# Mamba-2 block on one core: GpSimd's product of conv and D moves ahead of xs, and the decays' subtractions are split in two in the first and last group

## The chip, the cores and the metric

The kernel runs on one core of a Trainium2 chip. The metric is device time in microseconds (us), the median of several executions. TensorE is called PE, VectorE DVE, ScalarE ACT and GpSimd POOL, as in the profile; SP issues most transfers.

## The reference, cut to what matters

The model has two layers; the change lies in the first, a Mamba-2 mixer of 8 groups with 8 heads each:

```python
zxbcdt = u @ in_proj
xbc = silu(causal_depthwise_conv(xbc, conv_w, conv_b))   # x, B and C of the group
a = d * A; cum = cumsum(a)
seg = cum[:, :, None] - cum[:, None, :]
decay = where(causal, exp(where(causal, seg, 0.0)), 0.0)
cb = einsum("bign,bjgn->bijg", c, b)
y_intra = einsum("bijg,bijgr,bjgr,bjgrp->bigrp", cb, decay, d, x)
y_inter = einsum("bign,bgrpn,bigr->bigrp", c, state, exp(cum))
to_end = exp(cum[:, -1:] - cum) * d
y = y_intra + y_inter + D_skip[:, :, None] * xs
g = y * silu(z)                                          # then a group norm and out_proj
```

256 tokens are two chunks of 128. An MLP, a differential attention and another MLP follow and are not touched.

## The kernel before, in words

All large products are made of weights that stream in as slabs of 128x1024 float32. SP loads slab `s` into one of four `raw` buffers; ACT copies its high part (`split`, L622), DVE subtracts it from the original to get the low part (`split`, L912), and PE makes three matmuls for each pair of tiles (`three`, L1445 to L1447). PE takes 24 matmuls of 256 columns for a slab. There are four split buffers (`LEAD`), so ACT may start slab `s` once PE has finished slab `s - 4`, and SP may refill a `raw` buffer once DVE has split it.

The order of everything is written by hand. Each engine goes through the same list of steps `(unit, i)`, one slab a step; at step `k` ACT and DVE first split slab `k + 4` and then do the step's other work (`steps`, `mix_step`); PE multiplies slab `k` and then does the step's other work. An engine runs its own list strictly in order. What a step's other work waits for is a semaphore.

A group's steps are xs (8 slabs), bc (4), z (8) and acc (8, `out_proj` of the group before). The first group has no acc, and the last has z ahead of acc. Where z comes right behind bc (`z_first`), the chain of one group is this, by step:

- (xs, 7) and (bc, 3): DVE's `convolve` of xs and of bc (L1215, L1219); in the first group that of xs is done at (bc, 1). ACT's silu of xs (L769) raises `silu_done` the first time, its silu of bc at (z, 0) (L774) the second.
- (z, 1): DVE's 16 subtractions for the decays (L1245), then `seg_done`.
- (z, 3): PE's `spread` (L1604, L1609) waits for both silus and turns xs; ACT copies it out (L787, `xs_ready`). DVE then makes `bt` and `cbm` (L1254, L1255) and raises `cb_ready`.
- POOL: `xd = xs * dt` for two chunks (L569), `xe` (L575), `yg = conv * D` (L579), then `pool_ready`.
- (z, 4): ACT's exponentials of the decays; DVE's products with `cbm` (L1262).
- (z, 6): PE's product for the state (L1666) waits for `cb_ready` and `pool_ready`. (z, 7): PE's products within the chunk (L1674) and from the state (L1678).

In the six groups of the loop the 16 subtractions stand at (xs, 4), ACT's exponentials at (acc, 3), and `spread` at (acc, 7), where PE also waits for DVE's sum of (acc, 5) (L992, `acc_added`).

Of the kernel before, what the change touches and what calls it, by code (L numbers as in the profile page):

```python
# [25 lines left out]
ALU = mybir.AluOpType  # L26
# [5 lines left out]
S = 256  # L32
MT = S // P
DI = 2 * D
G = 8
# [151 lines left out]
def column_bcast(ap, n):  # L187

    return ap.unsqueeze(2).to_broadcast([ap.shape[0], ap.shape[1], n])
# [7 lines left out]
def build(nc, w, out):  # L197
# [41 lines left out]
    with ctx:  # L239
# [54 lines left out]
        conv = mb("conv", [P, 6, S])  # L294
        xs = mb("xs", [P, MT, BLK])
        xd = mb("xd", [P, MT, BLK])
        xe = mb("xe", [P, BLK])
        yg = mb("yg", [P, 4, S])
# [16 lines left out]
        dcol = mb("dcol", [P, NH // 2])  # L315
# [56 lines left out]
        pre_ready, conv_done, silu_done = sem("pre_ready"), sem("conv_done"), sem("silu_done")  # L372
# [114 lines left out]
        @block.gpsimd  # L487
        def _(pool):
            chain = Tally(pool, pool_chain)
            g_ = nc.gpsimd  # L490

            g_.memset(pre[:, :, 0:TAPS - 1], 0.0)
            g_.memset(ones[:, :], 1.0)
            chain.mark(g_.memset(ident[:, :], 0.0))
            chain.mark(g_.memset(causal[:, :], 1.0))
            chain.wait()
            g_.affine_select(out=ident[:, :], in_=ident[:, :], compare_op=ALU.not_equal, fill=1.0, base=0,
                             pattern=[[-1, P]], channel_multiplier=1)

            g_.affine_select(out=causal[:, :], in_=causal[:, :], compare_op=ALU.is_ge, fill=0.0, base=0,  # L500
                             pattern=[[1, P]], channel_multiplier=-1).then_inc(consts_ready, 1)

            pool.wait_ge(x_in[PIECES - 1], 16)
            for i, name in enumerate(("a_dt_bias", "a_A_log", "a_D")):
                pool.dma_start(hd[:, i, :], w[name][0].partition_broadcast(P)).then_inc(heads_in, 16)
            for i, name in enumerate(("b_lambda_q1", "b_lambda_k1", "b_lambda_q2", "b_lambda_k2")):
                pool.dma_start(lamv[:, i, :], w[name][0].partition_broadcast(P)).then_inc(lam_in, 16)
            pool.dma_start(relrow[:, :], w["rel_bias"].rearrange("b h -> h b"), allow_slow_non_contiguous=True)\
                .then_inc(rel_in, 16)


            pool.wait_ge(rel_in, 16)
            bounds = bucket_bounds()
            g_.memset(bias_row[:, 0:P], MASKED)
            for b in range(BUCKETS):
                lo, hi = P + bounds[b], P + bounds[b + 1]
                last = g_.tensor_copy(bias_row[:, lo:hi], relrow[:, b:b + 1].to_broadcast([HEADS, hi - lo]))
            chain.mark(last)
            chain.wait()

            pool.dma_start(bias_dram, bias_row[:, :]).then_inc(bias_out, 16)

            def zero_y(r):
                pool.wait_ge(x_lo, KT // 2 * (r + 1))
                for nt in range(NT):
                    last = g_.memset(y[:, :, nt * BLK:(nt + 1) * BLK], 0.0)
                last.then_inc(y_zeroed, 1)

            def next_postw(r, vec):
                pool.wait_ge(yw_ready, NT * r)  # L530
                pool.dma_start(postw[:, :], vec.partition_broadcast(P)).then_inc(postw_in, 16)

            def sum_squares(g):

                pool.wait_ge(g_sq, g)
                chain.mark(g_.tensor_tensor(out=zs[:, 0:2, :], in0=zs[:, 0:2, :], in1=zs[:, 2:4, :], op=ALU.add))
                chain.wait()
                g_.tensor_tensor(out=zs[:, 0, :], in0=zs[:, 0, :], in1=zs[:, 1, :], op=ALU.add).then_inc(g_added, 1)

            def group(g):  # L540

                if above(g):
                    pool.wait_ge(silu_done, 2 * g)
                for lo, n, at0 in ((0, 4, g * 4), (4, 1, 32 + g), (5, 1, 40 + g)):
                    for tp in range(TAPS + 1):
                        col = P * (1 + tp // 2) + 48 * (tp % 2)
                        last = g_.tensor_copy(cpar[:, tp, lo:lo + n], par[:, bass.ds(col + at0, n)])
                last.then_inc(cpar_ready, 1)
                if above(g):
                    pool.wait_ge(ecb_ready, g)  # L550
                else:
                    pool.wait_ge(expd_ready, 1)
                g_.tensor_copy(gcum[:, :, :], cum[:, :, bass.ds(g * R, R)]).then_inc(gcum_ready, 1)
                if not above(g):
                    pool.wait_ge(cumt_ready, 1)
                    pool.dma_start(cum_dram, cumt[:, :]).then_inc(cum_out, 16)
                    pool.wait_ge(cum_out, 16)

                src = cum_dram[bass.ds(g * R, R), :].rearrange("r s -> (r s)").partition_broadcast(P)
                pool.dma_start(cumb[:, :, :].rearrange("p r s -> p (r s)"), src).then_inc(cumb_in, 16)  # L560

                if above(g):
                    sum_squares(g)
                pool.wait_ge(xs_ready, g + 1)
                if above(g):
                    pool.wait_ge(h_ready, g)
                chain.mark(g_.tensor_copy(gpar[:, :], par[:, bass.ds(80 + g * 4, 4)]))
                for c in range(MT):
                    last = g_.tensor_tensor(  # L569
                        out=xd[:, c, :].rearrange("p (r d) -> p r d", r=R), in0=xs[:, c, :].rearrange("p (r d) -> p r d", r=R),  # L570
                        in1=column_bcast(dt[:, c, bass.ds(g * R, R)], PD), op=ALU.mult)
                    chain.mark(last)
                    if c == 0:
                        chain.wait()
                        g_.tensor_tensor(out=xe[:, :].rearrange("p (r d) -> p r d", r=R),  # L575
                                         in0=xd[:, 0, :].rearrange("p (r d) -> p r d", r=R),
                                         in1=column_bcast(todend[:, bass.ds(g * R, R)], PD),
                                         op=ALU.mult)
                g_.tensor_tensor(out=yg[:, :, :], in0=conv[:, 0:4, :], in1=column_bcast(dcol[:, bass.ds(g * 4, 4)], S),  # L579
                                 op=ALU.mult).then_inc(pool_ready, 1)  # L580

            pool.wait_ge(par_ready, 2)
            group(0)
            pool.dma_start(postw[:, :], w["norm_post_mix"][0].partition_broadcast(P)).then_inc(postw_in, 16)
            zero_y(0)
            with pool.Fori(0, G - 1) as t:
                chain.enter(t, 4)
                group(t + 1)
            chain.leave(G - 1, 4)
            sum_squares(G)  # L590
            next_postw(1, w["norm_post_mlp"][0])
            zero_y(1)
            next_postw(2, w["norm_post_mix"][1])

            def tab_load(g):

                src = bass.AP(tensor=bias_dram.tensor, offset=g * (HG * (P + S)) + 1,
                              ap=[[1, P], [P + S, HG], [1, S]])
                pool.dma_start(tab[:, :, :], src).then_inc(tab_in, 16)

            pool.wait_ge(bias_out, 16)
            pool.wait_ge(h_new, 2 * H_STEPS)
            tab_load(0)
            zero_y(2)
            with pool.Fori(0, QG - 1) as t:
                pool.wait_ge(lg_ready, HG * (t + 1))
                tab_load(t + 1)
            next_postw(3, w["norm_post_mlp"][1])
            zero_y(3)
# [295 lines left out]
        def _(dve):  # L905
            chain = Tally(dve, dve_chain)
# [320 lines left out]
            def mix_step(first, g, unit, i):  # L1227
# [6 lines left out]
                    block_lo(*((last_b if unit == "acc" else (bhi[0], blo[0]))))  # L1234
                if (unit, i) == ("xs", 6) and not first:
                    gate_factor(g)
                if (unit, i) == (("z", 1) if z_first else ("xs", 4)):

                    dve.wait_ge(cumb_in, 16 * (g + 1))
                    dve.wait_ge(gcum_ready, g + 1)  # L1240
                    if not first:
                        dve.wait_ge(y_done, g)
                    for c in range(MT):
                        for r in range(R):
                            last = ve.tensor_scalar(m[:, c, r, :], cumb[:, r, c * P:(c + 1) * P], gcum[:, c, r:r + 1], 0.0,  # L1245
                                                    ALU.subtract, ALU.min)
                    last.then_inc(seg_done, 1)
                if (unit, i) in (("xs", 7), ("bc", 3)) and not (first and unit == "xs"):
                    convolve(first, g, unit)
                if unit == "acc":  # L1250
# [613 lines left out]
```

## Time and profile before

| | |
|---|---|
| median of 3 runs | 2555.12 us (2554.38 to 2555.68) |
| the profiled execution's own time | 2554.14 us |
| its span (first to last instruction) | 2552.5 us |
| PE busy | 2519.7 us, 99% of the span |
| DVE, ACT, POOL busy | 1800.7, 1220.8 and 154.8 us |
| mixer, first group | to about 94 us; each looped group takes 84 us |

The time outside the span is 1.6 us. A busy share says little here: what counts is where PE stands still, and at which granted clock it works (PEclk, 1.00 is 2.4 GHz and 0.50 is 1.2 GHz).

### The profile page before, as it was taken

What the parts mean: (1) busy time and instruction counts of PE and PEld (TensorE: products, weight loads), DVE (VectorE), ACT (ScalarE), POOL (GpSimd) and SP (SyncE); (2) the same over time, 40 slices, a digit from 0 to 9 for tenths busy, and PEclk for the clock granted to TensorE, in tenths of its full rate; (3) what the DMA queues carried; (4) which work ended last, traced back from release to release, by engine and by line L of the source; (5) the groups of instructions that cost most, each with busy time, mean ns of one, the idle gap of its engine ahead of it and who ended that gap; (6) DMA issues with size and microseconds to landing.
All of it is one profiled execution on the core that took longest, in us unless ns stands there. A gap on an engine that the chain in (4) does not pass through costs nothing.

```text
span 2552.5 us, 45617 instructions
## 1 busy us (share of the span) xinstructions
PE 2519.7 (99%) x17261; PEld 2320.2 (91%) x17261; DVE 1800.7 (71%) x2580; ACT 1220.8 (48%) x1597; POOL 154.8 (6%) x269
## 2 busy tenths in 40 slices
PE   8999999999999999999999999999999999999997
PEld 7999999999899989899998998998899999989896
DVE  6878777887886565666666876778866666565667
ACT  6555545554554343434444654455644444343433
POOL 2222022202100000000000000000000000000000
PEclk9999999999999999999999999999999999999999
DMA  7666656656556666666666555555566666666664
GB/s 198 198 203 190 181 179 201 196 174 189 176 173 198 190 190 189 191 192 186 193 181 197 188 176 174 176 172 167 177 192 188 192 182 197 189 190 189 191 191 135
DMA packets 267579, 474.14 MB, mean 186 GB/s; under 512 B 16625, under 2 KB 50530, under 8 KB 265954
## 3 DMA queue, kind: packets, MB, share of 16 engines
q1 hardware_dynamic: 264818, 457.92, 59.3%
q0 software_dynamic: 2624, 15.00, 1.9%
q8 instruction: 57, 0.93, 0.1%
q14 instruction: 32, 0.26, 0.0%
q10 hardware_dynamic: 48, 0.02, 0.0%
HBM read 470.70 MB, written 2.19 MB: 185 GB/s over the span
## 4 chain that ended last, share of the span: by engine, by line
PE 96%; DVE 2%; ACT 1%; issue 0%; DMA 0%; SPq 0%; DVEq 0%; ACTq 0%
PE ps L1445 31%; PE ps L1446 31%; PE ps L1447 31%; PE ps L1674 1%; DVE whl L912 1%; PE ps L1546 0%; PE ps L1762 0%; PE ps L1678 0%; ACT whl L622 0%; DMA h<-x 0%; DVE m L1245 0%; PE ps L1604 0%; PE ps L1666 0%; DVE conv L1219 0%; PE ps L1574 0%
## 5 line engine op out<-in xcount | busy, mean ns | idle before, releaser
L912 DVE TENSOR_TENSOR whl<-raw,whl 128x1024 fp32r<-128x1024 f32 x865 | 1071.4, 1239 | 689.7 <-ACT whl L622 677.2
L622 ACT ACTIVATE whl<-raw 128x1024 fp32r<-128x1024 f32 x865 | 916.5, 1060 | 1173.7 <-PE ps L1447 1165.3
L1445 PE MATMUL ps<-xhl,whl 128*128 128x256 f32 x3588 | 1011.7, 282 | 3.9 <-DVE whl L912 2.0
L1446 PE MATMUL ps<-xhl,whl 128*128 128x256 f32 x3588 | 1001.9, 279 | 0.0
L1447 PE MATMUL ps<-xhl,whl 128*128 128x256 f32 x3588 | 1001.3, 279 | 0.0
L1445 PEld LDWEIGHTS ps<-xhl,whl 128*128 128x128 f32 x3588 | 674.5, 188 | 8.6 <-DVE whl L912 2.2
L1446 PEld LDWEIGHTS ps<-xhl,whl 128*128 128x128 f32 x3588 | 674.6, 188 | 3.1 <-issue 1.9
L1447 PEld LDWEIGHTS ps<-xhl,whl 128*128 128x128 f32 x3588 | 674.3, 188 | 0.0
L1445 PE MATMUL ps<-whl,bhl 128*128 128x512 f32 x1320 | 512.9, 389 | 0.0
L1446 PE MATMUL ps<-whl,bhl 128*128 128x512 f32 x1320 | 512.3, 388 | 0.0
L1447 PE MATMUL ps<-whl,bhl 128*128 128x512 f32 x1320 | 511.9, 388 | 0.0
L1447 PEld LDWEIGHTS ps<-whl,bhl 128*128 128x128 f32 x1320 | 247.8, 188 | 51.3
L1445 PEld LDWEIGHTS ps<-whl,bhl 128*128 128x128 f32 x1320 | 247.9, 188 | 50.1
L1446 PEld LDWEIGHTS ps<-whl,bhl 128*128 128x128 f32 x1320 | 247.8, 188 | 49.5
L996 DVE TENSOR_TENSOR y<-y,ps 128x1024 f32<-128x1024 f32 x141 | 172.1, 1221 | 7.3 <-PE ps L1447 2.5
L823 ACT ACTIVATE bhl<-relu 128x512 fp32r<-128x512 f32 x64 | 36.9, 625 | 83.2 <-DVE relu L1295 83.2
L1445 PE MATMUL ps<-khl,whl 128*128 128x256 f32 x256 | 72.7, 284 | 0.0
L1446 PE MATMUL ps<-khl,whl 128*128 128x256 f32 x256 | 71.5, 279 | 0.0
L1447 PE MATMUL ps<-khl,whl 128*128 128x256 f32 x256 | 71.4, 279 | 0.0
L1445 PE MATMUL ps<-whl,khl 128*128 128x512 f32 (+1 forms) x164 | 64.0, 390 | 0.0
L1447 PE MATMUL ps<-whl,khl 128*128 128x512 f32 (+1 forms) x164 | 63.1, 385 | 0.0
L1446 PE MATMUL ps<-whl,khl 128*128 128x512 f32 (+1 forms) x164 | 63.0, 384 | 0.0
(224 smaller groups left out, 1677.8 us busy)
## 6 DMA issues: line engine op xcount, KB each, us to landing
raw<-mlp_w SPq DMA_DIRECT2D x512, 512.0 KB, 4.2
raw<-a_in_proj SPq DMA_DIRECT2D x161, 512.0 KB, 4.5
raw<-a_out_proj SPq DMA_DIRECT2D x64, 512.0 KB, 4.2
raw<-b_w_q SPq DMA_DIRECT2D x32, 512.0 KB, 3.7
raw<-w_k SPq DMA_DIRECT2D x32, 512.0 KB, 4.0
raw<-w_v SPq DMA_DIRECT2D x32, 512.0 KB, 3.7
raw<-b_out_proj SPq DMA_DIRECT2D x32, 512.0 KB, 3.7
cumb<-cum_scratch POOLq DMA_DIRECT2D x8, 1024.0 KB, 7.7
```

The lines of the kernel that those rows point to most:

```text
L622: sc.activation(whi[:, s.split, lo:lo + SLAB], raw[:, s.raw, :], ACT.Copy).then_inc(hi_ready, 1)
L823: last = sc.activation(bhi[which][:, 2 * n:2 * n + 2, :].rearrange("p f s -> p (f s)"), relu[:, n, :], ACT.Square)
L912: ve.tensor_tensor(out=wlo[:, s.split, lo:lo + SLAB], in0=raw[:, s.raw, :], in1=whi[:, s.split, lo:lo + SLAB].bitcast(F32), op=ALU.subtrac ...
L996: ve.tensor_tensor(out=cols, in0=cols, in1=ps[:, bank:bank + 2, :], op=ALU.add).then_inc(acc_added, 1)
L1445: te.matmul(outs, lh, rh, start=start, stop=False, skip_group_check=True)
L1446: te.matmul(outs, lh, rl, start=False, stop=False, skip_group_check=True)
L1447: return te.matmul(outs, ll, rh, start=False, stop=stop, skip_group_check=True)
L1674: te.matmul(ps[r % 2 * PD:(r % 2 + 1) * PD, 5 + r // 4, col:col + P], xd[:, c, r * PD:(r + 1) * PD], m[:, c, r, :], start=True, stop=True, ...
```

## The change

Two things. POOL makes `yg = conv * D` as soon as the silu of xs is done, ahead of its wait for `xs_ready`; `pool_ready` is now raised by the second `xd`. And where z comes right behind bc (first and last group), DVE makes the eight subtractions of chunk 0 at (z, 1) and those of chunk 1 at (z, 2), so one slab split stands between them.

```diff
@@ POOL, group(g)
-                pool.wait_ge(xs_ready, g + 1)
+                pool.wait_ge(silu_done, 2 * g + 1)
                 if above(g):
                     pool.wait_ge(h_ready, g)
+                g_.tensor_tensor(out=yg[:, :, :], in0=conv[:, 0:4, :], in1=column_bcast(dcol[:, bass.ds(g * 4, 4)], S), op=ALU.mult)
+                pool.wait_ge(xs_ready, g + 1)
                 chain.mark(g_.tensor_copy(gpar[:, :], par[:, bass.ds(80 + g * 4, 4)]))
...
-                    chain.mark(last)
                     if c == 0:
+                        chain.mark(last)
                         chain.wait()
...
-                g_.tensor_tensor(out=yg[:, :, :], in0=conv[:, 0:4, :], in1=column_bcast(dcol[:, bass.ds(g * 4, 4)], S),
-                                 op=ALU.mult).then_inc(pool_ready, 1)
+                last.then_inc(pool_ready, 1)
@@ DVE, mix_step
-                if (unit, i) == (("z", 1) if z_first else ("xs", 4)):
+                if (unit, i) in ((("z", 1), ("z", 2)) if z_first else (("xs", 4),)):
...
-                    for c in range(MT):
+                    for c in (i - 1,) if z_first else range(MT):
...
-                    last.then_inc(seg_done, 1)
+                    if c == MT - 1:
+                        last.then_inc(seg_done, 1)
```

POOL's queue in the first group, `-` before and `+` changed (`yg`, `gpar`, `xd`, `xe` are the tiles written, `postw` the norm weights loaded next):

```order
-L567 COPY gpar<-par 128x4
-L569 TENSOR_TENSOR xd<-xs,dt 128x512
-L575 TENSOR_TENSOR xe<-xd,todend 128x512
-L569 TENSOR_TENSOR xd<-xs,dt 128x512
-L579 TENSOR_TENSOR yg<-conv,dcol 128x1024
-L584 DMA postw<-norm_post_mix 128x2048
+L567 TENSOR_TENSOR yg<-conv,dcol 128x1024
+L569 COPY gpar<-par 128x4
+L571 TENSOR_TENSOR xd<-xs,dt 128x512
+L577 TENSOR_TENSOR xe<-xd,todend 128x512
+L571 TENSOR_TENSOR xd<-xs,dt 128x512
+L585 DMA postw<-norm_post_mix 128x2048
```

The product `yg` stands first instead of last. The same move is made in every group of the loop.

DVE's queue in the first group before, from the slab split of step (z, 1) on:

```order
L912 TENSOR_TENSOR whl<-raw,whl 128x1024
L1245 TENSOR_SCALAR m<-cumb,gcum 128x128 x16
L912 TENSOR_TENSOR whl<-raw,whl 128x1024 x2
L1254 COPY bt<-ps 128x128
L1255 TENSOR_TENSOR cbm<-ps,causal 128x256
```

And changed (its lines are one or two further down):

```order
L913 TENSOR_TENSOR whl<-raw,whl 128x1024
L1246 TENSOR_SCALAR m<-cumb,gcum 128x128 x8
L913 TENSOR_TENSOR whl<-raw,whl 128x1024
L1246 TENSOR_SCALAR m<-cumb,gcum 128x128 x8
L913 TENSOR_TENSOR whl<-raw,whl 128x1024
L1256 COPY bt<-ps 128x128
L1257 TENSOR_TENSOR cbm<-ps,causal 128x256
```

The first of the two splits behind the subtractions now stands in their middle; the second, and `cb_ready` behind it, keep their place.

## Rows read from the trace of the kernel before

**Rows 1.** The page: the span, and its part 1.

```profile
span 2552.5 us, 45617 instructions
PE 2519.7 (99%) x17261; PEld 2320.2 (91%) x17261; DVE 1800.7 (71%) x2580; ACT 1220.8 (48%) x1597; POOL 154.8 (6%) x269
```

**Rows 2.** Waits of PE, 14 to 700 us: total, times, longest.

```profile
PE ps L1445 <- DVE whl L912: 2.0, 1, 2.0
PE ps L1445 <- DVE xhl L1007: 1.1, 1, 1.1
```

**Rows 3.** Windows: busy time of each engine, PEclk, DMA share, GB/s.

```profile
14.70:17.00 2.30, 1.12 (x8) 0.64 (x6) 1.52 (x4) 2.27 (x5) 0.24 (x1) 1.00 1.09 110
79.90:82.20 2.30, 0.26 (x3) 0.06 (x1) 2.27 (x3) 1.10 (x1) 2.30 (x3) 1.00 0.02 4
...
83.00:86.40 3.40, 3.40 (x18) 3.40 (x17) 3.33 (x6) 3.37 (x5) 3.40 (x6) 0.50 0.90 311
```

**Rows 4.** The chain that ended last, 79 to 93 us: start, us.

```profile
82.20 0.38 PE ps L1445
...
86.84 0.86 PE ps L1666 x2
90.52 1.90 PE ps L1674 x32
```

**Rows 5.** Timeline of DVE, first group: start, us, engine, line, operation.

```profile
67.16 0.62 DVE L1215 TENSOR_SCALAR conv<-pre,cpar 128x256 f32<-128x256 f32 x2
...
73.47 7.54 DVE L1245 TENSOR_SCALAR m<-cumb,gcum 128x128 f32<-128x128 f32 x16
80.94 2.47 DVE L912 TENSOR_TENSOR whl<-raw,whl 128x1024 fp32r<-128x1024 f32 x2
...
83.65 0.41 DVE L1255 TENSOR_TENSOR cbm<-ps,causal 128x256 f32<-128x256 f32 x1
```

**Rows 6.** The same timeline in narrow stretches: two single subtractions.

```profile
75.66 1.13 DVE L1245 TENSOR_SCALAR m<-cumb,gcum 128x128 f32<-128x128 f32 x1
79.03 1.99 DVE L1245 TENSOR_SCALAR m<-cumb,gcum 128x128 f32<-128x128 f32 x1
```

**Rows 7.** Timeline of POOL, first group.

```profile
75.63 1.08 POOL L569 TENSOR_TENSOR xd<-xs,dt 128x512 f32<-128x512 f32 x1
...
78.99 1.95 POOL L579 TENSOR_TENSOR yg<-conv,dcol 128x1024 f32<-128x1024 f32 x1
```

**Rows 8.** Timelines of ACT and PE, first group, with the idle time ahead.

```profile
64.99 1.71 ACT L769 ACTIVATE conv<-conv,cpar 128x256 f32<-128x256 f32 x4
...
70.25 0.91 ACT L774 ACTIVATE conv<-conv,cpar 128x256 f32<-128x256 f32 x2 [2.60 <-DVE conv L1219]
71.07 3.22 ACT L622 ACTIVATE whl<-raw 128x1024 fp32r<-128x1024 f32 x3
...
72.91 0.60 PE L1604 MATMUL ps<-ident,conv 128*128 128x128 f32 x4
```

**Rows 9.** Timeline of DVE, last group.

```profile
640.32 3.23 DVE L1245 TENSOR_SCALAR m<-cumb,gcum 128x128 f32<-128x128 f32 x16
```

**Rows 10.** Timelines of ACT, DVE and PE, first group of the loop.

```profile
133.95 0.91 ACT L774 ACTIVATE conv<-conv,cpar 128x256 f32<-128x256 f32 x2 [2.04 <-DVE conv L1219]
...
138.57 1.06 ACT L622 ACTIVATE whl<-raw 128x1024 fp32r<-128x1024 f32 x1 [1.64 <-PE ps L1447]
...
147.91 1.41 DVE L992 SCALAR_TENSOR_TENSOR y<-ps,stat,y 128x512 f32<-128x512 f32 x2
...
148.96 0.39 PE L1447 MATMUL ps<-whl,bhl 128*128 128x512 f32 x1
149.45 1.09 PE L1604 MATMUL ps<-ident,conv 128*128 128x128 f32 x8
```

**Rows 11.** Timelines of POOL and DVE behind that, where yg stood.

```profile
156.23 2.87 POOL L579 TENSOR_TENSOR yg<-conv,dcol 128x1024 f32<-128x1024 f32 x1
...
157.28 2.91 DVE L912 TENSOR_TENSOR whl<-raw,whl 128x1024 fp32r<-128x1024 f32 x1
```

More of the change, by code:

```diff
@@ L586, in _ @@
             with pool.Fori(0, G - 1) as t:
-                chain.enter(t, 4)
+                chain.enter(t, 3)
                 group(t + 1)
-            chain.leave(G - 1, 4)
+            chain.leave(G - 1, 3)
             sum_squares(G)
```

## The prediction

> **What bounds the kernel now.** The page comes first: PE is busy for 2519.7 of 2552.5 us [rows 1], so only PE's standing still, or its clock, has anything to give. The sum of PE's waits in the mixer is read next: there is one behind a slab split (DVE, L912), of 2.0 us, and no other of note after the start [rows 2]. The windows around it show a second loss. PE is busy for 0.26 of the 2.30 us before 82.2, and from 83.0 to 86.4 its granted clock is 0.50, that is 1.2 GHz [rows 3]. The chain gives the price: slab z6 starts at 82.20 and gives way to the state's product at 86.84, 4.64 us; that product takes 0.86, and slab z7 then needs 90.52 - 87.70 = 2.82 us at full clock [rows 4]. The slow clock costs 4.64 - 2.82 = 1.8 us. The stall costs 2.30 - 0.26 = 2.04 us of idle, and an estimated 0.16 more, because matmuls overlap and the next would have begun before the last one's end: 2.2. So **4.0 us** is what the first group can give back.
>
> Why is the split late? DVE's 16 subtractions take 7.54 us in the first group [rows 5], and 3.23 us in the last [rows 9]: 0.20 us each where nothing disturbs them. Single ones show the reason. One issued at 75.66 takes 1.13 us, one issued at 79.03 takes 1.99 [rows 6], and beside them POOL's xd began at 75.63 and yg at 78.99 [rows 7]. Each ends just after the POOL instruction does. So DVE stands still behind a POOL product: 0.86 us of DVE's time for one of 512 columns, 1.7 for yg (its next subtraction starts at 80.94 instead of 79.23). Three products of 512 columns (xd, xe, xd) and yg make 3 x 0.86 + 1.7 = 4.3 us, what lies between 3.23 and 7.54.
>
> **The change, part by part: first group.** Taken at its word it removes 1.7 us of blocking and moves a split ahead of eight subtractions. But yg doesn't vanish. It now starts when ACT's silu of xs is done, at 66.70 (64.99 + 1.71) [rows 8]. DVE is then in a split that ends at 67.13, and at 67.16 come the convolution's two L1215 [rows 5], of the same kind as the subtractions.
>
> The Trainium skill ("SBUF — State Buffer", the shared port pair) says that the pair is an exclusive lock held for the whole instruction, for a DVE instruction in a two-port mode or with two SBUF inputs against a POOL one that reads SBUF. By that rule yg has a price wherever it lies under such DVE work, and moving it only chooses the victim. The rows above agree for L1245 and L912; none shows the lock for the convolution.
>
> I therefore bound yg's price for the convolution from both sides: nothing, if yg slips between, and 1.95 us, its own length. I take 1.7, since L1215 is nearest to the subtractions. With that, in order:
>
> - DVE's convolution of bc, ACT's silu of bc behind it and ACT's three slab splits [rows 8] come 1.7 us later. PE's `spread` at 72.91 [rows 8] waits for that silu, now done at 71.16 + 1.7 = 72.86: 0.1 us lost at most.
> - POOL's first xd moves from 75.63 [rows 7] to 77.3, since ACT copies xs behind the three splits. Its three products, 1.08 to 1.2 us each with the wait between, and 0.6 for a DVE split that holds the first, run to 81.3.
> - DVE splits slab z5 by 75.1 (ACT's part of it is done at 73.8), does eight subtractions undisturbed (8 x 0.20) by 76.8, and splits z6 by 78.0. PE wants z6 at 80.1: the stall and the slow clock are gone.
> - The other eight run under xd, xe and xd: 8 x 0.20 + 3 x 0.86 = 4.2, to 82.1. Slab z7's split follows to 83.3, `cbm` and `cb_ready` to 84.0 (now 84.06 [rows 5]; the same).
> - PE finishes z6 at 82.9 and waits for `cb_ready`, some **1.1 us**. What was late is still late; it is only asked for one slab later. The product ends at 84.9, slab z7 at 87.75, where L1674 starts; before it started at 90.52. Gain **2.8 us**.
> - The exponentials start at 82.2 instead of 81.1. Both products with `cbm` are ready by 87.6, just ahead of PE, and the state's copy by 89.5, ahead of L1678 at 89.65. Both covers are thin, under 0.2 us.
>
> Does the new 1.1 us wait cost clock? Between 14.7 and 17.0 PE waited 1.1 us for L1007 [rows 2], in a stretch at 1.00 [rows 3]; after 2.04 us of idle it fell. I take no fall.
>
> **The loop, six groups.** The same 1.7 us hit the convolution of bc. ACT waits 2.04 us for it, and after two slab splits waits 1.64 us for PE [rows 10]: that 1.64 is the cover. What is beyond it delays the exponentials, the splits behind them and DVE's sum L992, which ends at 149.32. PE ends its last slab matmul at 149.35 and starts `spread` at 149.45 [rows 10], so there is no cover left. Each group loses 1.7 - 1.64 = 0.06 us, six of them **0.4 us**. At the bounds it is nothing (block below 1.64) or 6 x 0.3 = 1.9 (block of 1.95). If a block were total for yg's 2.87 us as its row in the loop has it [rows 11], it would be 6 x 1.23 = 7.4.
>
> What yg leaves behind gives nothing there: the split at 157.28 that took 2.91 us [rows 11] will take 1.2, but PE waited for nothing there.
>
> **The last group.** No POOL product meets the subtractions (3.23 us for 16 [rows 9]), PE has no wait there [rows 2], and the split between changes only the order. The subtractions of chunk 1 may now slip under xd, by up to 3 x 0.86 = 2.6 us; ACT's exponentials and PE's later slabs leave over 1 us beyond that. Nothing.
>
> **Sum.** -2.8 + 0.4 = -2.4 us. Against the profiled execution's 2554.14 us that is 2551.7. It lies 1.0 below the median of 2555.12, and the after time is a median too: **2552.7 us**.
>
> **The rivals.** About 0.2% (5.1 us) is what a measurement of this kernel can tell from no change.
>
> - The whole 4.0 us comes back: yg slips through without holding the convolution, or `cb_ready` is ready in time. Without the block, DVE starts the subtractions at 73.47 as now and is through `cbm` by 82.2, before PE's 82.8. For it: no row shows the convolution blocked. Against: L1215 is the subtractions' kind. 2551.1 us, 0.2.
> - The clock falls again behind the new wait, since only one row of 1.1 us speaks against it: 1.8 us go back, 2554.5 us, 0.15.
> - The work only moves: the wait for `cb_ready` or for the products with `cbm` grows to what the stall was, or the loop leaks 0.3 to 0.4 us a group. 2555 us, 0.15.
> - Slower: the convolution in the loop is held for yg's whole 2.87 us. From a block of 1.64 + 2.8/6 = 2.1 us on, the loop takes more than the first group gives; at 2.87 it is -2.8 + 7.4 = +4.6, 2559.7 us. Against it: of those 2.87 us POOL itself spent one waiting for DVE, as the split issued at 157.28, which lost only 2.91 - 1.2 = 1.7, shows. 0.07.
>
> **How the numbers follow.** My forecast has 0.43; with block and waits off by a few tenths its own range is 2551.9 to 2553.8. The range for all goes to the full gain below and to the case where the work only moves above, with a little for the measurement's own spread of 1.3 us: 2550.8 to 2555.5. What is left out is the slower rival and the tails. Faster by over 0.2% means below 2550.0, more than the whole loss in the first group: 0.03. Slower by over 0.2% means above 2560.2: 0.04, the far end of the slower rival. The same: 0.93.
>
> **What would show it.** In the trace after: yg at 66.8 and an L1215 of about 2 us beside it; PE without its 2.04 us wait for L912, in its place about 1.1 us ahead of L1666 with POOL and ACT as described; PEclk 1.00 from 80 to 90; L1674 at 87.7; the looped groups 84.0 us apart, with ACT's 1.64 us gone and `spread` no more than 0.1 us later. It would be wrong if the convolution's block isn't near 1.7 us, if the clock falls again, or if the thin covers before L1674 and L1678 fail.

## The result and the profile after

The changed kernel takes 2560.47 us in the median of 13 runs (2558.66 to 2562.49), the kernel before 2554.44 us in 13 (2552.63 to 2555.68): 6.0 us more, a ratio of 1.0023 with a 95% interval of 1.0015 to 1.0032. The profiled execution took 2561.45 us, 7.3 more than that of before.

The page of the changed kernel, its span and part 1, beside [rows 1]:

```profile
span 2559.8 us, 45625 instructions
PE 2523.2 (99%) x17261; PEld 2323.0 (91%) x17261; DVE 1807.7 (71%) x2580; ACT 1220.7 (48%) x1597; POOL 148.6 (6%) x269
```

The waits of PE from 14 to 700 us (total, times, longest), beside [rows 2]:

```profile
PE ps L1668 <- DVE cbm L1257: 4.6, 1, 4.6
PE ps L1447 <- DVE y L993: 1.9, 6, 0.3
PE ps L1447 <- DVE xhl L1008: 1.2, 1, 1.2
```

The 2.0 us behind a slab split are gone. In their place the state's product (now L1668) waits 4.6 us for `cbm`, and there are six waits of 0.3 us, one in each looped group. The windows (busy PE, PEld, DVE, ACT, POOL, then PEclk, DMA share, GB/s), beside [rows 3]:

```profile
83.30:87.10 3.80, 0.01 (x1) 0.00 (x0) 3.80 (x5) 0.97 (x1) 3.80 (x7) 1.00 0.56 233
87.30:94.00 6.70, 6.11 (x22) 5.07 (x23) 6.30 (x7) 5.97 (x8) 4.96 (x13) 0.50 0.66 209
...
1469.70:1473.00 3.30, 3.30 (x18) 3.30 (x17) 1.79 (x3) 0.00 (x0) 1.41 (x2) 0.50 0.33 94
```

The clock fell at 87.2, before the longer wait was over, and stayed at 0.50 for 6.8 us where it had been 3.4. It fell once more at 1469.6, ahead of the attention, where the profile of before shows no fall. Ahead of that second fall PE had waited 2.4 us, as it does in the kernel before (before, then changed):

```profile
PE ps L1580 <- DVE diag L957: 2.4, 1, 2.4
...
PE ps L1582 <- DVE diag L958: 2.4, 1, 2.4
```

Why is `cbm` (the masked product of C and B, which the state's product waits for through `cb_ready`) late? The timeline of DVE in the changed kernel, beside [rows 5, 6]:

```profile
66.22 1.23 DVE L913 TENSOR_TENSOR whl<-raw,whl 128x1024 fp32r<-128x1024 f32 x1
67.48 2.13 DVE L1216 TENSOR_SCALAR conv<-pre,cpar 128x256 f32<-128x256 f32 x2
...
75.31 1.66 DVE L1246 TENSOR_SCALAR m<-cumb,gcum 128x128 f32<-128x128 f32 x8
76.88 1.22 DVE L913 TENSOR_TENSOR whl<-raw,whl 128x1024 fp32r<-128x1024 f32 x1
78.14 7.91 DVE L1246 TENSOR_SCALAR m<-cumb,gcum 128x128 f32<-128x128 f32 x8
85.97 1.21 DVE L913 TENSOR_TENSOR whl<-raw,whl 128x1024 fp32r<-128x1024 f32 x1
87.22 0.29 DVE L1256 COPY bt<-ps 128x128 f32<-128x128 f32 x1
87.43 0.41 DVE L1257 TENSOR_TENSOR cbm<-ps,causal 128x256 f32<-128x256 f32 x1
```

And a narrow stretch of it at 81.7 to 82:

```profile
81.34 4.33 DVE L1246 TENSOR_SCALAR m<-cumb,gcum 128x128 f32<-128x128 f32 x2
```

POOL in the same stretch, beside [rows 7]:

```profile
67.11 2.09 POOL L567 TENSOR_TENSOR yg<-conv,dcol 128x1024 f32<-128x1024 f32 x1 [3.05 <-ACT conv L770]
...
78.11 1.04 POOL L571 TENSOR_TENSOR xd<-xs,dt 128x512 f32<-128x512 f32 x1
79.23 1.10 POOL L577 TENSOR_TENSOR xe<-xd,todend 128x512 f32<-128x512 f32 x1
80.30 1.04 POOL L571 TENSOR_TENSOR xd<-xs,dt 128x512 f32<-128x512 f32 x1
81.28 0.60 POOL L585 DMA_DIRECT2D postw<-norm_post_mix  x1
81.87 3.64 POOL L526 MEMSET y<- 128x1024 f32 x4
```

Until 81.3 everything runs as forecast to within 0.2 us: the first eight subtractions undisturbed, the split of z6 done at 78.1, four more by 81.4. Then two subtractions, issued at 81.34 and 81.53, stay unfinished until 85.6, and the last two follow them. Beside them stand POOL's four memsets of `y`. In the kernel before, the same memsets stood here:

```profile
81.47 3.65 POOL L526 MEMSET y<- 128x1024 f32 x4
```

The last subtraction had ended at 81.02, half a microsecond before that row, and DVE was in its slab splits by then.

### The profile page after: what moved, and what is told of

Read it like the earlier page. It is cut to its first block, busy times and chain, and to the rows that moved or that the text cites. A ratio compares the mean times of both kernels' runs of the same rounds, so it can differ in the third digit from the quotient of the medians.

```text
span 2559.8 us, 45625 instructions
## 1 busy us (share of the span) xinstructions
PE 2523.2 (99%) x17261; PEld 2323.0 (91%) x17261; DVE 1807.7 (71%) x2580; ACT 1220.7 (48%) x1597; POOL 148.6 (6%) x269
## 4 chain that ended last, share of the span: by engine, by line
PE 94%; DVE 4%; ACT 1%; issue 1%; DMA 0%; DVEq 0%; SPq 0%; ACTq 0%
PE ps L1447 30%; PE ps L1448 30%; PE ps L1449 30%; DVE whl L913 1%; PE ps L1676 1%; ACT whl L623 1%; PE ps L1548 0%; PE ps L1764 0%; DVE y L993 0%; PE ps L1680 0%; DVE m L1246 0%; PE ps L1668 0%; DMA h<-x 0%; DVE conv L1220 0%; PE ps L1576 0%
```

## The experiments

Theory M: the memsets hold DVE's subtractions. Theory Y, which was also the forecast's term for the loop: the earlier yg holds the convolution of bc, and that is late downstream. Rivals stand in each expectation. The edits are against the changed kernel unless said otherwise. e1 to e4 are compared with one set of 31 runs of before (median 2554.43 us), e5 to e8 with another of 33 (2554.10). The state's product is L1666 of the kernel before, and L1674's place that of the product within the chunk, whatever their line numbers in a variant.

| kernel | `spread`, start | state's product | L1674's place | from `spread` to it | a looped group | median against before |
|---|---|---|---|---|---|---|
| before | 72.91 | 86.67 | 90.45 | 17.5 | 83.95 | |
| changed | 73.23 | 87.89 | 94.60 | 21.4 | 84.23 | +6.0 |
| e1 | 72.88 | 83.69 | 87.55 | 14.7 | 84.25 | -0.9 |
| e2 | 72.91 | 87.71 | 93.97 | 21.1 | 83.96 | +4.7 |
| e3 | 73.81 | 91.03 | 94.78 | 21.0 | 84.23 | +7.1 |
| e4 | 74.32 | 85.13 | 88.99 | 14.7 | 83.96 | -1.7 |
| e5 | 73.24 | 83.33 | 87.16 | 13.9 | 83.95 | -2.3 |
| e6 | 73.15 | 84.12 | 87.98 | 14.8 | 83.95 | -1.3 |
| e7 | 73.24 | 84.64 | 88.49 | 15.3 | 84.24 | -0.3 |
| e8 | 72.87 | 85.77 | 91.23 | 18.4 | 84.24 | +4.1 |

Starts are those of the timelines, in us; the looped group is the middle one of five distances between two `spread`s, which lie within 0.2 of each other. The 95% intervals of e1, e4, e6 and e7 include no change; the changed kernel, e2, e3 and e8 are slower than before beyond them, and e5 is faster. What holds what is read from the times in the traces, not from the medians.

**e1, the memsets wait.**

```diff
+            pool.wait_ge(seg_done, 1)
             zero_y(0)
```

> The changed kernel, but POOL waits for all 16 subtractions of the first group (seg_done) before its four memsets of y; the DMA of postw is still issued ahead of that wait. Theory M (the memsets hold DVE's last four subtractions from 81.5 to 85.6 us): they end near 82.1, the state's product L1668 waits about 1.1 us instead of 4.6, PEclk stays 1.00 there, the first group is 2.8 us faster than before and the loop 1.6 slower: about 1.2 us below before. Rival D (the DMA of postw and its issue hold them): they still end near 86 and the time is that of the changed kernel, 6 us above before.

Median 2553.55 against 2554.43 us, ratio 0.9998 (0.9989 to 1.0007). DVE, a narrow stretch of it (81 to 81.8), and POOL in e1:

```profile
77.78 4.06 DVE L1247 TENSOR_SCALAR m<-cumb,gcum 128x128 f32<-128x128 f32 x8
81.76 1.21 DVE L914 TENSOR_TENSOR whl<-raw,whl 128x1024 fp32r<-128x1024 f32 x1
...
79.97 1.87 DVE L1247 TENSOR_SCALAR m<-cumb,gcum 128x128 f32<-128x128 f32 x5
...
80.92 0.60 POOL L585 DMA_DIRECT2D postw<-norm_post_mix  x1
81.91 3.63 POOL L526 MEMSET y<- 128x1024 f32 x4 [0.39 <-DVE m L1247]
```

The last eight subtractions take 4.06 us instead of 7.91 and end at 81.84, although POOL issues the DMA beside them: the first of the five in the narrow row is held by xd to 81.05, and the other four are through 0.8 us later. One added wait is worth 6.7 us in the first group. PE's wait for `cbm` is 0.7 us, and the clock stays at 1.00. Theory M holds; rival D falls.

**e2, DVE's part alone** (the kernel before, with the split subtractions).

> The kernel before with DVE's part of the change alone; POOL's yg stays last. The convolution and the loop are undisturbed: looped groups 83.95 us apart, as before. Eight subtractions end at 75.1, slab z6 is split by 76.3, the other eight meet xd, xe, xd and yg, and about three are left at 81.4. If only the memsets hold them (from 82.0 on) these three slip through in the 0.6 us of the DMA issue: cb_ready near 84, time 2 to 3 us below before. If the DMA issue holds them too, the memsets follow without a gap and they end near 86: a wait of 4 to 5 us before L1666, the clock falls, about 4 us above before.

2559.10 against 2554.43 us, ratio 1.0018 (1.0008 to 1.0027). DVE, the narrow stretch 81.7 to 82 of it, and POOL:

```profile
76.29 9.57 DVE L1245 TENSOR_SCALAR m<-cumb,gcum 128x128 f32<-128x128 f32 x8
...
81.35 4.33 DVE L1245 TENSOR_SCALAR m<-cumb,gcum 128x128 f32<-128x128 f32 x2
...
79.46 1.89 POOL L579 TENSOR_TENSOR yg<-conv,dcol 128x1024 f32<-128x1024 f32 x1
81.29 0.60 POOL L584 DMA_DIRECT2D postw<-norm_post_mix  x1
81.88 3.64 POOL L526 MEMSET y<- 128x1024 f32 x4
```

So the split alone, without yg's move, already runs into the memsets: a split's 1.2 us in the middle pushes the last subtractions over the edge. Three should have passed during the DMA's issue, and didn't; e1 shows that the issue itself doesn't stop them (four passed there, three of them issued within its 0.60 us). What holds is the memset queued right behind it, and it holds from some 0.5 us before its own row begins: the subtraction issued at 81.35, just as yg ends, is held already. So the half microsecond that the rows of the kernel before show between its last subtraction and the memsets was hardly room: here not one more subtraction got in behind yg. PE waits 4.7 us for `cbm`. The looped groups are those of before.

**e3, POOL's part alone** (one step of 16 subtractions again).

> The changed kernel with the 16 subtractions in one step again; yg first on POOL. By theory M ten subtractions end by 77.3, three or four more pass beside xd, xe and xd, and the last one or two are held by the memsets to 85.7. Slab z6's split then ends near 87, PE waits 7 us for it, the clock falls: first group 5 to 7 us slower than before, loop 1.6 slower, 7 to 9 us above before in all. If the memsets are not the cause: subtractions done near 81.6, about 2 us above before.

2561.49 against 2554.43 us, ratio 1.0027 (1.0017 to 1.0037). As expected, the last subtraction is held, and the split of z6 behind it. But PE waits 4.8 us for it, not 7, and the first group takes 3.4 us more than before, not 5 to 7. The reason stands in a narrow stretch of DVE:

```profile
81.45 4.30 DVE L1246 TENSOR_SCALAR m<-cumb,gcum 128x128 f32<-128x128 f32 x1
81.65 4.10 DVE L913 TENSOR_TENSOR whl<-raw,whl 128x1024 fp32r<-128x1024 f32 x1
```

The slab split ends at 85.75 together with the subtraction, instead of 1.2 us after it.

**e4, yg first in the first group only**, with e1's wait.

```diff
-                pool.wait_ge(silu_done, 2 * g + 1)
+                if not above(g):
+                    pool.wait_ge(silu_done, 1)
+                    times_d()
+                pool.wait_ge(xs_ready, g + 1)
...
+                if above(g):
+                    last = times_d()
                 last.then_inc(pool_ready, 1)
```

> The changed kernel with the memsets behind the subtractions, and yg first in the first group alone; in the loop and the last group yg stays last, as before. Theory M and the theory that the loop's 1.6 us come from yg ahead of the convolution of bc: looped groups 83.95 us apart again, L1674 of the first group near 87.8 instead of 90.5, 2.8 us below before. Rival for the loop (its 1.6 us come from the shift in time, not from yg): the groups stay 84.2 apart and the time is 1.2 below before.

2552.76 against 2554.43 us, ratio 0.9994 (0.9985 to 1.0003). The looped groups return to 83.96 us; PE's six waits are gone. The loop's loss belongs to yg's place. The median is 1.7 us below before, not 2.8, and L1674's place is at 88.99, not 87.8. In this profile the clock fell near the start, behind a wait of 1.0 us at the place where before had waited 1.1 us at no cost [rows 2, 3], and everything after it came over a microsecond later (window 17 to 20.3):

```profile
17.00:20.30 3.30, 3.30 (x17) 3.30 (x17) 2.42 (x4) 2.60 (x5) 0.00 (x0) 0.50 0.66 35
```

**e5, POOL gives way** (against the kernel before; subtractions in one step; its other lines, DVE's wait for `yg_ready` among them, are left out).

```diff
                 if above(g):
                     pool.wait_ge(h_ready, g)
+                else:
+                    pool.wait_ge(seg_done, 1)
...
+                last.then_inc(pool_ready, 1)
...
-                                 op=ALU.mult).then_inc(pool_ready, 1)
+                                 op=ALU.mult).then_inc(yg_ready, 1)
```

> The kernel before, DVE's 16 subtractions in one step, but in the first group POOL waits for them (seg_done) before xd, xe, xd and yg; pool_ready is raised by the second xd and DVE waits for yg on a semaphore of its own. If POOL's instructions beside the subtractions are the whole cause of the first group's stall: 16 subtractions in 3.2 us, PE never waits there, from spread to L1674 13.5 us instead of 17.5, loop untouched: 4.0 us below before in a run where the clock fell, 2.2 in one where it didn't. Rival: POOL's late products hold DVE's slab splits and the state's product waits for pool_ready instead: 1 to 2 us come back.

2551.77 against 2554.10 us, ratio 0.9989 (0.9980 to 0.9998): the lowest median of all.

```profile
73.80 3.23 DVE L1249 TENSOR_SCALAR m<-cumb,gcum 128x128 f32<-128x128 f32 x16
76.95 3.35 DVE L916 TENSOR_TENSOR whl<-raw,whl 128x1024 fp32r<-128x1024 f32 x2
...
82.32 4.78 DVE L1266 TENSOR_TENSOR m<-m,cbm 128x1024 f32<-128x1024 f32 x2
...
79.29 1.91 POOL L578 TENSOR_TENSOR xe<-xd,todend 128x512 f32<-128x512 f32 x1
81.17 2.02 POOL L572 TENSOR_TENSOR xd<-xs,dt 128x512 f32<-128x512 f32 x1
83.15 2.87 POOL L583 TENSOR_TENSOR yg<-conv,dcol 128x1024 f32<-128x1024 f32 x1
```

The 16 subtractions take 3.23 us. POOL's products now meet slab splits and `cbm`'s products and both lose time, but PE waits for neither. 3.6 of the first group's 4.0 us come back.

**e6, e2 with e1's wait.**

> DVE's part of the change alone (yg last everywhere), with the memsets of y behind the first group's subtractions. Against e2 it shows the memsets' share without yg's move, and against e4 what yg's move is worth in the first group. Theory: the same 14.7 us from spread to L1674 as e1 and e4, loop as before, time that of e4 (1.7 below before). Rival (yg ahead of xs is what makes e1 and e4 fast): yg still holds one subtraction for 1.7 us, L1674 comes 1.5 us later and the time is that of before.

2552.77 against 2554.10 us, ratio 0.9993 (0.9984 to 1.0002). From `spread` to L1674's place 14.8 us, against 14.7 in e4: the move of yg is worth 0.2 us in the first group, next to nothing. Ahead of xs it takes 1.5 us from the convolution (the two instructions of L1215's place last 2.13 us in e4, 0.62 in e6) and gives 1.7 to the last eight subtractions. Those in e4, then in e6:

```profile
79.23 4.06 DVE L1253 TENSOR_SCALAR m<-cumb,gcum 128x128 f32<-128x128 f32 x8
...
76.55 5.72 DVE L1246 TENSOR_SCALAR m<-cumb,gcum 128x128 f32<-128x128 f32 x8
```

**e7, another form of subtraction.**

```diff
+                            if first and c == 1:
+                                last = ve.scalar_tensor_tensor(out=m[:, c, r, :], in0=cumb[:, r, c * P:(c + 1) * P], scalar=gcum[:, c, r:r + 1],
+                                                               in1=zero[:, :], op0=ALU.subtract, op1=ALU.min)
+                                continue
```

> The changed kernel, memsets where they are, but the first group's last eight subtractions in a form with two inputs in SBUF (scalar_tensor_tensor against a tile of zeros), 0.27 us each where it was 0.20. Theory L (the memsets hold tensor_scalar because of its form, as they never held the slab splits, which have two inputs): they are held only by xd, xe and xd, end near 82.7, the state's product waits 1.6 us instead of 4.6, the clock doesn't fall there, from spread to L1674 15.2 us instead of 21.4; time near before, 0.5 us above e1. Rival (the memsets hold any DVE instruction that writes beside them, or POOL's queue is late for another reason): the wait stays at 4.6 us or grows.

2553.80 against 2554.10 us, ratio 1.0001 (0.9992 to 1.0010).

```profile
78.14 4.65 DVE L1249 SCALAR_TENSOR_TENSOR m<-cumb,gcum,zero 128x128 f32<-128x128 f32 x8
...
81.87 3.65 POOL L528 MEMSET y<- 128x1024 f32 x4
```

With the memsets where they are, the slower form needs 4.65 us and the faster one 7.91. 4.65 is what e1 took without memsets, 4.06, and the form's own 8 x 0.07. PE's wait is 1.3 us, the clock stays up. Theory L holds. The Trainium skill ("SBUF — State Buffer", on the shared port pair) says just this: a DVE instruction with two SBUF inputs contends with a POOL instruction that reads SBUF, not with one that only writes it, while one in a two-port mode contends with any. The trace agrees on both halves, if `tensor_scalar` runs in a two-port mode here, which no run shows: the same eight subtractions beside the same memsets, 4.65 and 7.91 us.

**e8, half the dose.**

```diff
+                    if r == 0 and nt == 2:
+                        pool.wait_ge(seg_done, 1)
                     last = g_.memset(y[:, :, nt * BLK:(nt + 1) * BLK], 0.0)
```

> The changed kernel with two of the four memsets of y behind the first group's subtractions, two where they were: half the dose. Theory M: the subtractions are held from 81.4 to about 83.8 instead of 85.6, the state's product waits 2.8 us instead of 4.6, the clock still falls (2.04 us of idle were enough before). Time 2 to 4 us below the changed kernel. Rival (a hold that does not scale with the memsets): 4.6 us as in the changed kernel or 0.7 as in e1.

2558.15 against 2554.10 us, ratio 1.0015 (1.0006 to 1.0024). With two memsets ahead of the wait the eight subtractions take 6.14 us, between 4.06 with none and 7.91 with four, and PE waits:

```profile
77.78 6.14 DVE L1248 TENSOR_SCALAR m<-cumb,gcum 128x128 f32<-128x128 f32 x8
...
PE ps L1670 <- DVE cbm L1259: 2.8, 1, 2.8
```

The hold goes by the memsets. The clock fell for 3.4 us. The median is 2.3 us below that of the changed kernel.

## Why the prediction was wrong

**The step that failed** is the fourth of the first group: "The other eight run under xd, xe and xd: 8 x 0.20 + 3 x 0.86 = 4.2, to 82.1. Slab z7's split follows to 83.3, `cbm` and `cb_ready` to 84.0." They took 7.91 us and `cb_ready` came at 87.8. I followed POOL's queue as far as its last product and no further. The DMA behind it was in the order shown ahead of the prediction; the four memsets were not, though the trace of before had them right behind the DMA (81.47, above). Of a queue that moves against another one, all of it counts. With the memsets out of the way (e1) the step's own arithmetic holds: 4.06 us, `cbm` 0.7 us late where 1.1 was forecast, 2.9 us gained where 2.8 was.

**The slower rival** gave 2559.7 us, close to 2560.5, but that is luck, since its mechanism isn't there: in the loop yg held the convolution for 1.6 us, near what I took, not for 2.87.

**Point by point.** yg's price for the convolution, taken as 1.7 us from its nearest row: right, at 1.5 to 1.6. The pair of L1216 ahead of which yg starts lasts 2.13 us in the first group (above) and 2.25 in the first looped one (below), where the row of before has 0.62 [rows 5]. That the times up to 81.3 us fit to 0.2 is in part luck, since this hold was 0.2 us shorter than taken and the start 0.3 us later. No clock fall for a wait near 1.1 us: in the first group waits of 0.7 to 1.3 us cost none (e1, e4, e6, e7), those of 2.8 us and more did. But the row that the forecast took it from is no rule: at the same place near the start e4's clock fell behind 1.0 us. Nor is "after 2.04 us of idle it fell": the kernel before also waited 2.4 us for L957, and its clock stayed at 1.00. The last group, nothing: right. From the last looped group's `spread` to the last group's L1674 it is 86.72 us in both kernels.

**The loop's term was mis-sized:** 0.4 us, measured 1.7. The place was wrong too. I had read the cover at ACT's 1.64 us and put the wait at `spread`. The first looped group of the changed kernel shows an earlier one (DVE, then PE):

```profile
135.07 2.25 DVE L1216 TENSOR_SCALAR conv<-pre,cpar 128x256 f32<-128x256 f32 x2 [0.22 <-DVE whl L913]
...
146.81 1.41 DVE L993 SCALAR_TENSOR_TENSOR y<-ps,stat,y 128x512 f32<-128x512 f32 x2
...
148.36 0.49 PE L1447 MATMUL ps<-whl,bhl 128*128 128x512 f32 x1 [0.30 <-DVE y L993]
```

At (acc, 6) PE waits for the sum of (acc, 3). Before, these stood like this:

```profile
141.03 1.41 DVE L992 SCALAR_TENSOR_TENSOR y<-ps,stat,y 128x512 f32<-128x512 f32 x2
...
143.75 0.39 PE L1445 MATMUL ps<-whl,bhl 128*128 128x512 f32 x1
```

The sum ended at 142.44 and PE wanted it at 143.75: a cover of 1.3 us, for DVE's own queue, which carries the whole delay. The convolution starts at 135.07 instead of 130.92, 4.15 later, and the sum ends at 148.22, 5.78 later: 1.63 us of delay against 1.31 of cover leave 0.3, as the row says. Six times 0.3 is, to rounding, the 1.7 us.

**Where the time went,** profile against profile: start-up 0.3 (73.23 - 72.91), first group 3.8 (21.37 - 17.54), loop 1.7; the 1.5 that is left of the 7.3 us lies behind the mixer and goes with the clock's fall at 1469.6. From the last group's L1674 to the end of the run it is 1897.8 to 1898.0 us in the five profiles without such a fall and 1899.3 to 1899.7 in the five with one. In the medians the difference is 6.0.

**Left open.** Medians and first-group times don't add up to better than 1.4 us: e4, e5 and e6 have 2.9, 3.6 and 2.7 us less in the first group and no loss in the loop, and gain 1.7, 2.3 and 1.3 in the median. In their profiles a fall of the clock elsewhere takes what is missing: in e4 that at 16.9 us (`spread` starts 1.4 us later than before), in e5 and e6 one near 1460 us. Such a fall behind the wait for L957's place shows in the profiles of the changed kernel, e2, e3, e5 and e6, not in those of before, e1, e4, e7 and e8, and the wait is 2.4 us in all ten. Why the clock falls in some and not in others stays open. The runs that were not profiled have their mean granted clock on record to three places, too coarse to tell which falls came in them.

## What to carry to other kernels

When one engine's instruction can hold another's, follow both queues to the end of the stretch, memsets and DMA issues included: what looked 0.5 us clear of the stretch was what decided here, and the gap between two rows isn't room in which one more instruction gets through. Moving a POOL instruction out of the way only chooses whom it holds; making POOL wait until DVE's subtractions are through (e5) gave the shortest first group, 13.9 us from `spread` to L1674's place, with neither part of the change. And a delay has to be checked against the cover at every wait it passes on its way, the engine's own queue first, not just at the one whose idle time is printed.

## What was not expected of the hardware

- A memset of POOL that follows a DMA issue directly holds DVE's `tensor_scalar` from before its own row: the subtractions issued at 81.34 and 81.53 were held, the memset's row begins at 81.87 (in e2 two were held from 81.35 on, and the row begins at 81.88). With a semaphore wait between the two, four subtractions passed beside the same DMA issue (e1).
- Between xd, xe and xd a held subtraction gets through each time. Between four memsets none did, for 4.1 us.
- A slab split with two SBUF inputs that queues behind a held subtraction ends with it (e3: both at 85.75).
- In the first group idle times of 0.7 to 1.3 us cost no clock, 2.04 and 2.8 us cost 3.4 us at 0.50, and 4.6 to 4.8 us (changed kernel, e2, e3) cost 6.8 us, with the fall before the wait was over. But the length of a wait doesn't decide it alone: behind one of 2.4 us near 1460 us the clock fell in five of ten profiles, and near the start it fell behind 1.0 us in e4 and stayed at 1.00 behind 1.1 us in before.
